# Experts' up rows in another order: two k of w1, then two of w3, before they alternate

## The chip, the core and the metric

The kernel runs on one core of a Trainium2 chip. The metric is the device time of one execution in microseconds (us); shorter is better. The time before is the median of three runs.

## The reference

One inference step of a small hybrid encoder, two layers, in float32. There are 512 prompt tokens and 8 x 16 sample tokens, 640 in all, of width 1024. Each layer mixes tokens (an mLSTM, a sparse attention with an indexer, a causal pooling) and then has a feed-forward part. In the first layer that is one dense SwiGLU. In the second it is a choice of two out of eight SwiGLU experts for each token, and this is where the change is:

```python
def _swiglu(x, wa, wb, wc):
    return (jax.nn.silu(x @ wa) * (x @ wb)) @ wc

logits = (x @ w_router).astype(f32) + b_router.astype(f32)
top_v, top_i = lax.top_k(logits, TOP_K)
gates = jax.nn.softmax(top_v, axis=-1)
comb = jnp.sum(jax.nn.one_hot(top_i, N_EXPERTS, dtype=f32) * gates[..., None], axis=1)
for e in range(N_EXPERTS):
    y = y + comb[:, e:e + 1] * _swiglu(x, we1[e], we3[e], we2[e]).astype(f32)
```

`we1` and `we3` are 1024 x 1408 for each expert, `we2` is 1408 x 1024.

## The kernel before

The engines run programs of their own, tied by semaphores; their order is written out by hand. The tokens are sorted by expert into passes of 128 slots. A pass is one expert's weights with up to 128 tokens. The number of passes is known only at run time. The first two `up()` and the last two `down()` stand outside of the loop; each trip of the loop (13 trips with these inputs, `trips`) does `down()` of one pass and then `up()` of the pass two further on.

Weights come as rows. An up row is 128 x 1408 floats (704 KB): one k of the 1024 inputs, in eights of 128, of w1 or of w3. There are `UP_ROWS` = 16 of them, and c counts them; before, c = 2k + which, with which = 0 for w1 and 1 for w3. A down row is 128 x 1024 (512 KB), `DOWN_ROWS` = 11. Each row passes through these stations, at a place of a ring of `NPLACE` = 9:

- SyncE fetches it (`expert_rows`, L636 to L648) into `expert_ring` once the place is free (`expert_used`).
- ScalarE rounds it to its upper part (`upper`, `copy` at L1708), into `region_split` for places 0 to 5 and into `z_weights_upper` for places 6 to 8.
- VectorE subtracts, which gives the lower part (`lower`, `tt` at L2295), in `expert_lower`, and counts `expert_split`.
- TensorE uses it. `weight_parts()` waits for `expert_split` once at the head of a row. `product` makes three matmuls: upper by upper, upper tokens by lower weights, lower tokens by upper weights.

ScalarE and VectorE work `AHEAD` = 4 rows before TensorE in the order of the program: at TensorE's row c their programs have row c + 4. Since 27 rows make a trip and 27 is three times 9, each row of the loop has the same place in each trip: up row c = 0 is in place 7, c = 1 in place 8, c = 2 in place 0.

In `up()` (TensorE, L1536) an up row is cut into three parts of 512, 512 and 384 columns (`PARTS`), and part p of the w1 rows adds into PSUM bank p, of the w3 rows into bank 3 + p. All k of a bank add up there. The first row that writes a bank calls `claim(b)`, which waits until the bank's last reader is done (`holder`).

In `down()` (L1557) the results go to banks 6 and 7, and in between TensorE transposes the next pass's products: `turn_product` for part 0 into bank 3 after f = 4, for part 1 into bank 4 after f = 8, for part 2 into bank 5 after the last row. ScalarE copies each out of its bank (`upper_of_product`), then VectorE subtracts (`lower_of_product`, L2946) into `region_split` and counts `product_split`; that frees the bank. VectorE's order at the end of a `down()` is: row split of up row 2, `lower_of_product` of bank 4, row split of up row 3, `lower_of_product` of bank 5; then `up()` goes on with up row 4. A place in the ring is freed by the first matmul of the row that follows (`free_place`).

Of the kernel before, what the change touches and what calls it, by code (L numbers as in the profile page):

```python
# [10 lines left out]
KD = D // P  # L11
# [16 lines left out]
NF = FE // P  # L28
# [46 lines left out]
UP_ROWS, DOWN_ROWS = 2 * KD, NF  # L75
PASS_ROWS = UP_ROWS + DOWN_ROWS
assert PASS_ROWS % NPLACE == 0
PARTS = [(0, 512), (512, 1024), (1024, FE)]
TRIPS_AT = 31
CHUNK_DMAS = [len(w) for _, w in UP_CHUNKS] + [1] * len(W2_CHUNKS)  # L80
# [105 lines left out]
def build(nc, a, c, o, d):  # L186
# [11 lines left out]
    with ctx:  # L198
# [354 lines left out]
        def _(sp):  # L553
# [13 lines left out]
            def rows(w):  # L567
                return w.rearrange("(k p) n -> p k n", p=P)
# [26 lines left out]
            for l in range(DEPTH):  # L595
                w = rows(a["w_in"][l, :, :])
# [8 lines left out]
                w = rows(a["w_out"][l, :, :])  # L605
# [5 lines left out]
                for _ in range(2):  # L611
                    with sp.Fori(0, 2) as i:
                        n.enter(i, {"weights_used": EXPERT_CHUNKS})
                        q0 = slots.count["q"]
                        w1, w3 = (a[x][l // 2, :, :].rearrange("(k p) (e n) -> e p k n", p=P, e=2) for x in ("w1", "w3"))
                        w2 = a["w2"][l // 2, :, :].rearrange("(e k p) n -> e p k n", p=P, e=2)
                        w1, w3, w2 = (x[bass.ds(i, 1), :, :, :].rearrange("e p k n -> p (e k) n") for x in (w1, w3, w2))
# [20 lines left out]
            def expert_rows(e, up):  # L638

                nonlocal q  # L640
                w1, w3, w2 = (x[bass.ds(e, 1), :, :, :].rearrange("e p k n -> p (e k) n") for x in by_row)
                for src in [w[:, k, :] for k in range(KD) for w in (w1, w3)] if up else [w2[:, f, :] for f in range(NF)]:
                    if q >= NPLACE:
                        sp.wait_ge(expert_used, n.value("expert_used"))
                    n.add("expert_used")
                    place = q % NPLACE
                    q += 1
                    sp.dma_start(ER[:, place, 0:src.shape[1]], src).then_inc(expert_in[place], 16)  # L648
# [194 lines left out]
        def _(pe):  # L843
# [5 lines left out]
            def wait(s, value):  # L849
                pe.wait_ge(s, value)  # L850
# [4 lines left out]
            def claim(*banks):  # L855
                for b in banks:
                    if holder[b]:
                        wait(*holder[b])
                        holder[b] = None
# [56 lines left out]
            k = KD + 2 * DEPTH  # L916
# [108 lines left out]
            for l in range(DEPTH):  # L1025
# [71 lines left out]
                for k in range(KD):  # L1097
                    take(z_hidden_split)
                    for name, rows, banks, Wf in lead:
                        if k == 0:  # L1100
                            take(weights_split)
                        w = [x[:, k, 0:rows] for x in Wf]
# [9 lines left out]
                for kind, chunk, name, part, banks, who in UNITS[2:]:  # L1112
# [8 lines left out]
                    if kind == "f":  # L1121

                        for k in range(KD):
                            w = [x[:, k, part * P:part * P + rows] for x in Wf]
# [130 lines left out]
                for u in range(PAIR_UNITS + 3):  # L1255
                    if u < PAIR_UNITS:
                        pair, t = divmod(u, NTP)
                        w = P * (t + 1)
# [235 lines left out]
                if l % 2:  # L1494
# [11 lines left out]
                    def weight_parts():  # L1506

                        nonlocal place
                        take(expert_split)
                        at = place % NPLACE  # L1510
                        place += 1
                        return expert_upper(at), ERL[:, at, :]
# [12 lines left out]
                    def turn_product(part, bank):  # L1525

                        first, end = PARTS[part]
                        wait(product_made, n.value("product_made") - 2 + part)
# [7 lines left out]
                    def up():  # L1536

                        wait(rows_split, n.value("rows_split"))
                        for c in range(UP_ROWS):
                            k, which = divmod(c, 2)  # L1540
                            w = weight_parts()
                            for part, (first, end) in enumerate(PARTS):
                                b = 3 * which + part
                                if k == 0:
                                    claim(b)
                                begin, ins = product(PS[:, b, 0:end - first], [x[:, k, :] for x in (XGH, XGL)],
                                                     [x[:, first:end] for x in w], k == 0, k == KD - 1)
                                free_place(begin)
                                if k == KD - 1:
                                    ins.then_inc((gates_summed, ups_summed)[which], 1)  # L1550
                                    made = (silu_made, product_made)[which]
                                    holder[b] = (made, n.add(made.name))
                            release[0] = True
                            if c == 9:
                                turn_rows(0, 6)
# [24 lines left out]
                    for u, unit in enumerate(LATE_ROWS):  # L1580
                        b = u % 6
                        claim(b)
                        for j in range(4):
                            if unit[0] == "gates":
                                if u == NT * 2 - len(EARLY_ROWS) + 2 and j == 0:
                                    wait(gates_spread, 1)
                                k = 4 * unit[2] + j
# [47 lines left out]
                for it in range(4):  # L1635
# [35 lines left out]
                    for j, blocks in enumerate(W2_CHUNKS):  # L1671
                        c = len(UP_CHUNKS) + j
# [28 lines left out]
        def _(act):  # L1701
            n = Tally()

            def take(s, inc=1):
                act.wait_ge(s, n.add(s.name, inc))
# [135 lines left out]
            for l in range(DEPTH):  # L1841
# [273 lines left out]
                if l % 2:  # L2115
# [16 lines left out]
                    def upper_of_product(part, bank):  # L2132

                        first, end = PARTS[part]
                        take(product_turned)
# [3 lines left out]
                    def up(following):  # L2139

                        for c in range(UP_ROWS):
# [4 lines left out]
                            if c == 10:  # L2146
                                upper_of_rows(0, 6)
                        for part, (first, end) in enumerate(PARTS):
                            take(gates_summed)
# [115 lines left out]
        def _(dve):  # L2265
# [114 lines left out]
            for l in range(DEPTH):  # L2380
# [545 lines left out]
                if l % 2:  # L2926
# [19 lines left out]
                    def lower_of_product(part, bank):  # L2946

                        first, end = PARTS[part]
                        fs = slice(first // P, end // P)
# [4 lines left out]
                    def up(following):  # L2954

                        for c in range(UP_ROWS):
# [4 lines left out]
                            if c == 10:  # L2961
                                lower_of_rows(0, 6)
                        for part, (first, end) in enumerate(PARTS):
                            take(silu_made)
# [186 lines left out]
```

## Time and profile before

| | |
|---|---|
| median of three runs | 2340.25 us (2330.97 to 2342.22) |
| the profiled execution | 2339.32 us |
| its span, first to last instruction | 2337.5 us |
| granted clock of TensorE, mean | 0.933 |
| TensorE busy | 2148.8 us, 92% |
| VectorE busy | 1470.3 us, 63% |
| ScalarE busy | 1146.3 us, 49% |
| moved by DMA | 485.87 MB, 208 GB/s over the span |
| experts' weight rows | 240 of 704 KB, 165 of 512 KB |

A profile is of one execution, and its times are microseconds from the first instruction. The granted clock is TensorE's share of full speed, 1.0 for 2.4 GHz and 0.5 for 1.2 GHz. The experts take the time from about 1520 to 2290 us. Matmuls overlap each other, so a matmul's duration is longer than the distance from its start to the start of the next one.

### The profile page before, as it was taken

What the parts mean: (1) busy time and instruction counts of PE and PEld (TensorE: products, weight loads), DVE (VectorE), ACT (ScalarE), POOL (GpSimd) and SP (SyncE); (2) the same over time, 40 slices, a digit from 0 to 9 for tenths busy, and PEclk for the clock granted to TensorE, in tenths of its full rate; (3) what the DMA queues carried; (4) which work ended last, traced back from release to release, by engine and by line L of the source; (5) the groups of instructions that cost most, each with busy time, mean ns of one, the idle gap of its engine ahead of it and who ended that gap; (6) DMA issues with size and microseconds to landing.
All of it is one profiled execution on the core that took longest, in us unless ns stands there. A gap on an engine that the chain in (4) does not pass through costs nothing.

```text
span 2337.5 us, 36949 instructions
## 1 busy us (share of the span) xinstructions
PE 2148.8 (92%) x14013; PEld 1849.1 (79%) x14013; DVE 1470.3 (63%) x2156; ACT 1146.3 (49%) x1589; POOL 173.1 (7%) x257
## 2 busy tenths in 40 slices
PE   6999878898999999989998879889999999999996
PEld 4999634598999999989985448778888878888883
DVE  3567544255545454566675425578888888888885
ACT  5421235444434333343212444367777777777773
POOL 3000120110000000000000211100001000000101
PEclk7999679898999999999996889899999999999998
DMA  9222465624545455522231743199999999999995
GB/s 318 60 73 71 135 223 187 226 82 110 163 135 163 135 162 137 160 80 69 73 100 26 239 150 123 58 338 348 367 359 354 356 374 358 380 363 352 347 364 198
DMA packets 285982, 485.87 MB, mean 208 GB/s; under 512 B 21791, under 2 KB 216873, under 8 KB 285857
## 3 DMA queue, kind: packets, MB, share of 16 engines
q1 hardware_dynamic: 265536, 418.72, 52.1%
q0 software_dynamic: 20320, 65.39, 8.0%
q8 instruction: 90, 1.47, 0.3%
q14 instruction: 36, 0.29, 0.0%
HBM read 456.23 MB, written 26.97 MB: 207 GB/s over the span
## 4 chain that ended last, share of the span: by engine, by line
PE 76%; DMA 10%; DVE 6%; ACT 4%; issue 3%; SPq 1%; POOL 1%; ACTq 0%; PEldq 0%; DVEq 0%; PEld 0%; POOLq 0%
PE banks L871 72%; DMA expert_ring<-in_we 5%; PE banks L875 3%; DMA weight_ring<-in_w_ada 2%; ACT region_split L1708 1%; DVE scratch L2295 1%; DVE region L2295 1%; ACT scratch L1708 1%; DVE expert_lower L2295 1%; DMA mix_t<-region 1%; DMA region<-region 1%; SPq L565 1%; DMA scratch<-bias_rows 0%; DVE region_split L2295 0%; ACT hidden_t L1708 0%
## 5 line engine op out<-in xcount | busy, mean ns | idle before, releaser
L2295 DVE TENSOR_TENSOR expert_lower<-expert_ring,region_split 128x1408 fp32r<-128x1408 f32 (+1 forms) x270 | 388.3, 1467 | 27.0 <-ACT region_split L1708 17.3
L871 PE MATMUL banks<-upper_parts,region_split 128*128 128x320 f32 x1664 | 390.7, 310 | 4.5 <-DVE upper_parts L2295 4.5
L871 PE MATMUL banks<-upper_parts,weights_lower 128*128 128x320 f32 (+1 forms) x1248 | 387.2, 310 | 0.0
L871 PE MATMUL banks<-region_split 128*128 128x320 f32 (+1 forms) x1376 | 375.7, 336 | 1.7 <-DVE upper_parts L2295 1.7
L1708 ACT ACTIVATE region_split<-expert_ring 128x1408 fp32r<-128x1408 f32 (+1 forms) x270 | 331.8, 1257 | 61.4 <-DMA expert_ring<-in_we 61.3
L871 PE MATMUL banks<-region_split,upper_parts 128*128 128x512 f32 (+1 forms) x996 | 302.9, 380 | 1.4 <-DVE upper_parts L2295 1.4
L871 PEld LDWEIGHTS banks<-upper_parts,region_split 128*128 128x128 f32 x1664 | 285.1, 189 | 4.8 <-issue 4.8
L871 PE MATMUL banks<-expert_lower,upper_parts 128*128 128x512 f32 x720 | 271.0, 376 | 0.0
L871 PE MATMUL banks<-z_weights_upper,upper_parts 128*128 128x384 f32 (+1 forms) x764 | 238.3, 344 | 24.0 <-DVE region_split L2295 23.9
L871 PEld LDWEIGHTS banks<-region_split 128*128 128x128 f32 x1376 | 244.0, 188 | 18.2 <-DVE upper_parts L2295 1.5
L2295 DVE TENSOR_TENSOR expert_lower<-expert_ring,z_weights_upper 128x1024 fp32r<-128x1024 f32 (+1 forms) x135 | 192.2, 1442 | 73.9 <-ACT z_weights_upper L1708 71.5
L871 PEld LDWEIGHTS banks<-upper_parts,weights_lower 128*128 128x128 f32 (+1 forms) x1248 | 235.3, 189 | 0.0
L2295 DVE TENSOR_TENSOR weights_lower<-weight_ring,region_split 128x2048 fp32r<-128x2048 f32 (+2 forms) x72 | 168.9, 2350 | 96.2 <-ACT region_split L1708 96.2
L1708 ACT ACTIVATE region_split<-weight_ring 128x2048 fp32r<-128x2048 f32 (+2 forms) x72 | 140.6, 1958 | 164.2 <-PE banks L871 162.5
L1708 ACT ACTIVATE region<-banks 128x320 f32<-128x320 f32 (+3 forms) x185 | 83.7, 468 | 271.5 <-PE banks L871 267.4
L1708 ACT ACTIVATE z_weights_upper<-expert_ring 128x1024 fp32r<-128x1024 f32 (+1 forms) x135 | 166.7, 1237 | 101.0 <-DMA expert_ring<-in_we 100.5
L871 PEld LDWEIGHTS banks<-region_split,upper_parts 128*128 128x128 f32 x996 | 188.3, 191 | 31.7 <-DVE upper_parts L2295 1.8
L871 PE MATMUL banks<-region_split,weights_lower 128*128 128x320 f32 x608 | 187.9, 309 | 0.0
L871 PE MATMUL banks<-upper_parts,z_weights_upper 128*128 128x320 f32 (+1 forms) x544 | 171.1, 314 | 11.2 <-DVE hidden_lower_parts L2295 10.1
L871 PEld LDWEIGHTS banks<-z_weights_upper,upper_parts 128*128 128x128 f32 x764 | 143.3, 188 | 48.2 <-DVE region_split L2295 35.0
L871 PE MATMUL banks<-hidden_lower_parts,z_weights_upper 128*128 128x320 f32 (+1 forms) x544 | 169.9, 312 | 0.0
L871 PEld LDWEIGHTS banks<-expert_lower,upper_parts 128*128 128x128 f32 x720 | 137.2, 191 | 20.2
(317 smaller groups left out, 3254.8 us busy)
## 6 DMA issues: line engine op xcount, KB each, us to landing
expert_ring<-in_we SPq DMA_DIRECT2D x240, 704.0 KB, 8.2
expert_ring<-in_we SPq DMA_DIRECT2D x165, 512.0 KB, 4.5
weight_ring<-in_w_ada SPq DMA_DIRECT2D x48, 1024.0 KB, 9.0
weight_ring<-in_w SPq DMA_DIRECT2D x88, 512.0 KB, 4.9
weight_ring<-in_w_in SPq DMA_DIRECT2D x24, 1024.0 KB, 5.3
weight_ring<-in_w SPq DMA_DIRECT2D x16, 1408.0 KB, 6.5
weight_ring<-in_w_out SPq DMA_DIRECT2D x8, 1024.0 KB, 6.5
y_rows<-hidden_t POOLq DMA_DIRECT2D x15, 512.0 KB, 7.5
```

Source lines behind the costliest of these rows:

```text
L565: sp.dma_start(dst, src).then_inc(weights_in[q % NSLOT], 16)
L871: return nc.tensor.matmul(out, lhsT, rhs, start=first, stop=last)
L875: return nc.tensor.transpose(out, in_, ident[0:k, 0:k])
L1708: return nc.scalar.activation(out, in_, f, **kw)
L2295: return v.tensor_tensor(out, x, y, op)
```

## The change

`UP_ORDER` lists (k, which) for each c. Rows c = 1 and c = 2 of each `up()` change places: before, the first four rows were (0, w1), (0, w3), (1, w1), (1, w3); after, they are (0, w1), (1, w1), (0, w3), (1, w3). From c = 4 on nothing differs. SyncE fetches in the new order, and TensorE computes in it. The order of k within each bank stays.

```diff
+UP_ORDER = [(0, 0), (1, 0), (0, 1), (1, 1)] + [(k, which) for k in range(2, KD) for which in range(2)]
...
-                for src in [w[:, k, :] for k in range(KD) for w in (w1, w3)] if up else [w2[:, f, :] for f in range(NF)]:
+                for src in [(w1, w3)[which][:, k, :] for k, which in UP_ORDER] if up else [w2[:, f, :] for f in range(NF)]:
                     if q >= NPLACE:
                         sp.wait_ge(expert_used, n.value("expert_used"))
...
                         for c in range(UP_ROWS):
-                            k, which = divmod(c, 2)
+                            k, which = UP_ORDER[c]
                             w = weight_parts()
                             for part, (first, end) in enumerate(PARTS):
                                 b = 3 * which + part
```

## Rows read from the trace of the kernel before

**Rows 1.** Page, part 1: engine busy us, share of span, instructions.

```profile
PE 2148.8 (92%) x14013; PEld 1849.1 (79%) x14013; DVE 1470.3 (63%) x2156; ACT 1146.3 (49%) x1589; POOL 173.1 (7%) x257
```

**Rows 2.** Page, part 4: chain that ended last, share of span by line.

```profile
PE banks L871 72%; DMA expert_ring<-in_we 5%; PE banks L875 3%; DMA weight_ring<-in_w_ada 2%; ACT region_split L1708 1%; DVE scratch L2295 1%; DVE region L2295 1%; ACT scratch L1708 1%; DVE expert_lower L2295 1%; DMA mix_t<-region 1%; DMA region<-region 1%; SPq L565 1%; DMA scratch<-bias_rows 0%; DVE region_split L2295 0%; ACT hidden_t L1708 0%
```

**Rows 3.** Page, part 5: group, count | busy, mean ns | idle before, releaser.

```profile
L871 PE MATMUL banks<-z_weights_upper,upper_parts 128*128 128x384 f32 (+1 forms) x764 | 238.3, 344 | 24.0 <-DVE region_split L2295 23.9
```

**Rows 4.** TensorE's waits, 1600 to 2260 us: total us, times, longest.

```profile
PE banks L871 <- DVE region_split L2295: 23.9, 24, 1.3
```

**Rows 5.** Stretches, one per pass: length, busy (count) by engine, clock, DMA share, GB/s.

```profile
1621.45:1671.82 50.37, 48.45 (x233) 40.55 (x231) 43.03 (x36) 38.01 (x37) 3.71 (x4) 1.00 0.96 366
1671.82:1723.74 51.92, 49.99 (x232) 41.76 (x231) 43.92 (x36) 38.58 (x38) 3.70 (x4) 0.97 0.96 356
1723.74:1773.27 49.53, 48.43 (x233) 40.55 (x231) 42.41 (x36) 37.27 (x38) 3.69 (x4) 1.00 0.97 369
...
1823.37:1874.12 50.75, 48.43 (x233) 40.57 (x230) 43.25 (x36) 37.85 (x38) 3.71 (x4) 1.00 0.96 364
...
1924.69:1976.79 52.10, 49.89 (x230) 41.74 (x230) 44.55 (x36) 38.74 (x38) 3.69 (x4) 0.97 0.95 355
...
2177.39:2229.10 51.71, 50.02 (x233) 41.80 (x231) 42.54 (x36) 37.53 (x37) 3.69 (x4) 0.97 0.94 351
sum 607.65, PE 585.82 PEld 490.19 DVE 516.13 ACT 453.57 POOL 44.33; mean PE 48.82 PEld 40.85 DVE 43.01 ACT 37.80 POOL 3.69
```

**Rows 6.** TensorE's timeline: start, us, instruction [idle before <-releaser].

```profile
1621.45 0.48 PE L871 MATMUL banks<-z_weights_upper,upper_parts 128*128 128x512 f32 x1
...
1625.19 0.51 PE L871 MATMUL banks<-z_weights_upper,upper_parts 128*128 128x512 f32 x1 [0.89 <-DVE region_split L2295]
...
1627.19 0.45 PE L871 MATMUL banks<-z_weights_upper,upper_parts 128*128 128x384 f32 x1 [1.03 <-DVE region_split L2295]
...
1627.84 0.39 PE L871 MATMUL banks<-region_split,upper_parts 128*128 128x512 f32 x1
1628.06 0.40 PE L871 MATMUL banks<-expert_lower,upper_parts 128*128 128x512 f32 x1
...
1629.98 0.39 PE L871 MATMUL banks<-expert_lower,upper_parts 128*128 128x512 f32 x1
...
1728.65 0.44 PE L871 MATMUL banks<-z_weights_upper,upper_parts 128*128 128x384 f32 x1 [1.04 <-DVE region_split L2295]
...
1778.77 0.45 PE L871 MATMUL banks<-z_weights_upper,upper_parts 128*128 128x384 f32 x1 [1.04 <-DVE region_split L2295]
...
1827.49 0.49 PE L871 MATMUL banks<-z_weights_upper,upper_parts 128*128 128x512 f32 x1 [1.27 <-DVE region_split L2295]
...
1829.49 0.45 PE L871 MATMUL banks<-z_weights_upper,upper_parts 128*128 128x384 f32 x1 [1.05 <-DVE region_split L2295]
```

**Rows 7.** ScalarE's and VectorE's timeline in the first pass, same columns.

```profile
1621.49 1.39 ACT L1708 ACTIVATE region_split<-expert_ring 128x1408 fp32r<-128x1408 f32 x1 [0.36 <-DMA expert_ring<-in_we]
...
1622.91 1.62 DVE L2295 TENSOR_TENSOR expert_lower<-expert_ring,region_split 128x1408 fp32r<-128x1408 f32 x1
...
1624.45 0.68 DVE L2295 TENSOR_TENSOR region_split<-banks,region_split 128x512 fp32r<-128x512 f32 x1
...
1625.05 1.61 DVE L2295 TENSOR_TENSOR expert_lower<-expert_ring,region_split 128x1408 fp32r<-128x1408 f32 x1
...
1626.58 0.55 DVE L2295 TENSOR_TENSOR region_split<-banks,region_split 128x384 fp32r<-128x384 f32 x1
...
1627.27 6.23 DVE L2295 TENSOR_TENSOR expert_lower<-expert_ring,region_split 128x1408 fp32r<-128x1408 f32 x4
```

**Rows 8.** Other stretches, columns as in rows 5.

```profile
1678.00:1681.50 3.50, 3.50 (x11) 2.92 (x11) 3.50 (x3) 3.15 (x3) 0.00 (x0) 0.53 1.00 410
...
1773.00:1797.00 24.00, 22.30 (x107) 18.71 (x106) 22.12 (x16) 19.95 (x19) 0.59 (x1) 1.00 1.02 416
1797.00:1816.00 19.00, 19.00 (x92) 16.04 (x91) 17.81 (x18) 14.82 (x17) 3.10 (x3) 1.00 0.85 285
```

## The prediction

> **What bounds the kernel now.** I read the page first. TensorE is busy 92% of the span, VectorE 63%, ScalarE 49% [rows 1], and the chain that ended last runs 72% through the one matmul line L871, with 5% on the experts' weight DMAs [rows 2]. So the time is TensorE's, wherever TensorE has something to do, and a change pays only where TensorE stands still. Among the costliest groups one names such a place: matmuls that read `z_weights_upper` with `upper_parts` (the tokens' upper parts, so an up row, held in a ring place from 6 to 8) had 24.0 us of idle time before them, released by VectorE writing `region_split` [rows 3]. The list of waits says that this is all there is: in the stretch of the expert loop TensorE waits for one thing alone, 24 times, 23.9 us in total [rows 4].
>
> The next view is the table by stretches, cut at the first matmul of each `up()` of the loop. It gives twelve whole passes of the expert loop (a thirteenth `up()` follows at 2229.10), 607.65 us together, 50.6 us on average, with TensorE busy for 48 to 50 us of each, VectorE for 42 to 45 and the DMA share at 0.94 to 0.97 [rows 5]. TensorE is the bound, but the DMA share is what can spoil a gain, and I come back to it.
>
> The timeline of one pass shows the wait itself. The pass starts at 1621.45. A row without a wait takes 1.92 us (1628.06 to 1629.98, the same matmul in two rows that follow each other), so the third row should start at 1621.45 + 0.09 (the first matmul after the transposes is that much longer) + 2 x 1.92 = 1625.38. It starts at 1627.84 [rows 6]. The lost time, about 2.5 us, has two stops, both *within* row c = 1: one before the matmuls of its second part, which go on at 1625.19, and one before its third, at 1627.19 [rows 6]. A stop between parts of a row can't be a wait for that row's weights, since `weight_parts()` waits once at the head of the row. It is `claim(b)` for banks 4 and 5. Row c = 1 is k = 0 of w3, and it opens banks 3, 4, 5. Their last holder is `turn_product`, whose banks come free when ScalarE has copied and VectorE has subtracted (`lower_of_product`, `product_split`).
>
> VectorE's own timeline shows why it is late. It splits row 2 at 1622.91 (ScalarE rounded it from 1621.49 on, and had waited for the DMA), then `lower_of_product` for bank 4 at 1624.45 with 0.68 us (ends 1625.13, TensorE goes on at 1625.19), then row 3 at 1625.05 with 1.61 us, then `lower_of_product` for bank 5 at 1626.58 with 0.55 us (ends 1627.13, TensorE goes on at 1627.19) [rows 7]. The releases sit in VectorE's queue behind row splits, and the splits behind the DMA. They come at a time that TensorE's work on row c = 1 does not set.
>
> **The change part by part.**
>
> *SyncE's queue.* The second and the third row of each `up()` are fetched in the other order: (k 1, w1) before (k 0, w3). Both are 704 KB rows. The number, size, ring place and order of places are the same, and so are the waits. Nothing is moved past another queue. Cost: nothing.
>
> *ScalarE and VectorE.* They work by place. Their instructions are the same ones in the same order. Cost: nothing. Their deadlines change: until now TensorE reached row c = 2 only after the stops; now it reaches it earlier.
>
> *TensorE.* Row c = 1 now adds k = 1 of w1 into banks 0 to 2, already open, and claims nothing. Banks 3, 4, 5 are claimed in row c = 2. From c = 4 on all is as before, and each bank's k order stays. The claim of bank 5 moves from 0.09 + 1.92 + 1.39 = 3.40 us after the pass starts to 5.32 us (1.39 is two parts of three matmuls, at 0.23 each, as between 1628.06 and the next row). Bank 4's goes to 4.62.
>
> What stands against it is when the banks come free, counted from the pass's start: in the first pass 3.7 us for bank 4 and 5.7 for bank 5; in the worst of the thirteen, the one from 1823.37, 4.1 and 6.1; in the mildest kind, the one from 1723.74, bank 5 at 4.9 [rows 5, 6]. So bank 4 never stops TensorE again (4.1 against 4.6). Bank 5 still does in most passes, by 5.7 - 5.3 = 0.4 us in the usual one, 0.8 in the worst, nothing in the mildest. Over the thirteen I count 6 us, 0.45 us each. The stall shrinks; it doesn't go.
>
> Next in line are the weights. Row 2's split ends 1624.53, 3.1 us after the start, and TensorE will want it at 3.9. Row 3's ends at 5.2, wanted at 5.8 or later. Row 4's ends at 1627.27 + 1.62, which is 7.4, wanted at 8.2 [rows 7]. From there VectorE makes a row in 1.56 us (6.23 for four) and TensorE uses one in 1.92, so the distance grows. In the worst pass all of these are 0.4 us later and still in time, because bank 5 holds TensorE back by as much. So nothing new is waited for, by 0.4 us or more.
>
> *The sum.* A pass without a stop is 50.37 - 2.55 = 47.82 us (first pass, third row at 1627.84 in place of 1625.29 with 3.84 for two rows; the small 0.09 is in both). With the 0.45 us that stay it is 48.3. Twelve passes: 607.65 - 12 x 48.3 = 28 us saved. The thirteenth `up()` saves 2. Together 30 us. That holds a gift: three of the passes are 51.7 to 52.1 us long, as the one from 1671.82, and in each the granted clock falls to the lower level directly behind the two stops (a mean of 0.53 from 1678.0 to 1681.5, that is 1.2 GHz for nearly all of this stretch; it is the first of three such) [rows 5, 8]. Each fall costs about 1.6 us (51.92 against 50.37). With one stop of 0.4 us in place of two of about 1 us I expect fewer of them, but not surely none. If all three stay, the sum is 30 - 5 = 25 us. I take 28. The profiled execution had 2339.3 us, the median of the three runs is 2340.25, so nothing is to be rescaled: 2340.25 - 28 = 2312.
>
> *The first two `up()`* before the loop have no such wait in row c = 1: banks 3 to 5 were drained long before by other work. Bounds for this part: 0 to 1 us either way; I take 0.
>
> **The transfers, which could take it back.** A pass moves 366 GB/s x 50.37 us = 18.4 MB [rows 5]. In 48.3 us that is 382 GB/s. Is that to be had? In the stretch 1773 to 1797 the queues were full (share 1.02) and moved 416 GB/s; from 1797 to 1816 they moved 285 GB/s at a share of 0.85 [rows 8]. In this second stretch TensorE frees a place every 1.92 us and gets a 512 KB row for it, so the queues are fed slowly. That leaves 19 x (416 - 285) = 2.5 MB, 6 us of transfer, unused in each pass. A pass that is 2.1 us shorter takes 2 of these 6, and the backlog is gone before the next pass's first up rows are asked for. By this, 18.4 MB need 44.2 us, and TensorE's 48.3 stay the bound. The share of 0.96 overstates how near the limit is.
>
> The Trainium skill, "SBUF — State Buffer" (its summary of rules for kernel authors), says to reckon with about 358 GB/s between HBM and SBUF, because the HBM side binds; by that alone a pass of 18.4 MB would take 51 us and this change would bring nothing. The passes here already run at 351 to 369 GB/s and the full stretch at 416 [rows 5, 8], so the trace speaks against that figure as a limit for this core. The Trainium skill, "HBM Reference" (its specifications), gives about 425 GB/s for a core that streams alone; with that the trace agrees.
>
> **The rivals.**
>
> *A. The rows land later, in part.* With less slack in the queues the first up rows arrive perhaps 1 us later against TensorE, and both VectorE's releases and its splits with them. Then 1.4 us a pass stay in place of 0.45. For it: ScalarE waits for the DMA before nearly each row, and the DMA is full from before the pass's start. Against it: the pass from 1723.74 lasted only 49.5 us, and the bank 5 release of the one behind it, which started at 1773.27, was at 5.5 us (1778.77), no later than usual [rows 5, 6]. Time: 13 x 1 us given back, 2325.
>
> *B. The transfers are the bound.* If the mean pass of 50.6 us is what the queues need, TensorE's stops only move to the heads of rows. Against it are the 6 us unused, and passes of 49.5 to 50.4 us beside that mean. Time: 2340, no change. (By the Trainium skill's figure of 358 GB/s, "SBUF — State Buffer", this would be the case.)
>
> *C. Slower.* As B, but the waiting now comes in the middle of the row sequence, just where TensorE had run undisturbed, and the clock falls behind it in each pass and not in three. Price: ten more falls at 1.6 us, 2340 + 16 = 2356. It decides from the point where row 2's split comes over 2 us later than now (after 5.5 us rather than 3.1).
>
> *D. More than forecast.* The bank 5 stop goes altogether, if splits run a little earlier, and no clock fall is left: 30 + 6 = 36 us, 2304.
>
> That the change doesn't do what it says I hold for excluded by the place of the stops (between parts of a row, ending 0.06 us behind the VectorE instruction that frees the bank).
>
> **How the numbers follow.** Forecast (2306 to 2320): 0.66. A: 0.17. B: 0.06. C: 0.03. D: 0.08. The predicted time is 2312. The range goes from D, with the scatter of the runs (2331 to 2342) in mind, at 2301, to A with half a us more per pass, at 2330. What a measurement of this kernel can tell from no change is about 0.5%, 12 us: faster takes the forecast, D and nearly all of A, 0.90; within takes B and the rest of A, 0.07; slower is C, 0.03.
>
> **What would show it.** In the profile after: the 24 waits of TensorE for `region_split` become about 11 to 13, each of 0.2 to 0.8 us, now before a matmul that reads `region_split` weights (row 2 sits in place 0) and none in the second part; passes of about 48.3 us; GB/s over 375 in the passes; clock falls behind the stops rarer than three. Wrong is the step on the transfers if TensorE then waits at heads of rows for `expert_lower`, or if passes stay at 50 us; wrong is the bank step if two stops a pass remain.

## The result and the profile after

The changed kernel takes 2301.86 us (median of four, 2295.37 to 2306.12); beside it the kernel before took 2337.51 us (median of four). The ratio is 0.9833, with an interval of 0.9800 to 0.9865. The medians are 35.6 us apart (the ratio makes it 39) where 28 were forecast, and 2301.9 stands against 2312: the direction and the place were right, the size was too small by a fifth or more. The profiled execution took 2302.05 us, with a span of 2300.2.

The page first, part 1, the matmul group of rows 3, and then the list of TensorE's waits in the expert loop, as in rows 4 (total us, times, longest; the view lists stops of over 0.15 us):

```profile
PE 2128.3 (93%) x14013; PEld 1843.0 (80%) x14013; DVE 1465.5 (64%) x2156; ACT 1142.4 (50%) x1589; POOL 222.9 (10%) x257
...
L872 PE MATMUL banks<-z_weights_upper,upper_parts 128*128 128x384 f32 (+1 forms) x764 | 230.4, 339 | 0.1
```

```profile
PE banks L872 <- DVE region_split L2296: 0.6, 1, 0.6
```

The 24.0 us of idle time ahead of that group are 0.1. Of 24 waits [rows 4] one is left. Part 1 holds a second thing that I had not looked for: GpSimd is busy for 222.9 us, where it was 173.1 [rows 1], with the same 257 instructions.

The stretches between the first matmuls of the loop's `up()` (length, busy and count of PE, PEld, DVE, ACT, POOL, clock, DMA share, GB/s), to be held against rows 5:

```profile
1618.99:1667.75 48.76, 48.20 (x229) 40.60 (x230) 44.19 (x36) 38.31 (x38) 6.77 (x4) 1.00 0.97 373
1667.75:1715.62 47.87, 47.87 (x233) 40.69 (x231) 42.56 (x35) 38.12 (x39) 7.92 (x4) 1.00 0.98 382
...
2146.49:2194.36 47.87, 47.87 (x233) 40.69 (x231) 42.72 (x35) 37.24 (x38) 7.75 (x4) 1.00 0.98 381
sum 575.37, PE 574.82 PEld 488.09 DVE 513.28 ACT 451.73 POOL 94.32; mean PE 47.90 PEld 40.67 DVE 42.77 ACT 37.64 POOL 7.86
```

Eleven of the twelve passes are TensorE's own work and nothing else: 47.87 us long (47.86 to 47.91), 47.87 us busy, at full clock. The twelve together went from 607.65 to 575.37 us, 32.3 less. After the first matmul of the last `up()` come 105.8 us in place of 108.4, and before the first one 1619.0 in place of 1621.5. Together that is the 37.3 us between the two spans.

### The profile page after: what moved, and what is told of

The parts are those of the page before. It is cut to its first block, busy times and chain, and to the rows that moved or that the text cites. A ratio compares the mean times of both kernels' runs of the same rounds, so it can differ in the third digit from the quotient of the medians.

```text
span 2300.2 us, 36949 instructions
## 1 busy us (share of the span) xinstructions
PE 2128.3 (93%) x14013; PEld 1843.0 (80%) x14013; DVE 1465.5 (64%) x2156; ACT 1142.4 (50%) x1589; POOL 222.9 (10%) x257
## 4 chain that ended last, share of the span: by engine, by line
PE 83%; DVE 5%; DMA 5%; ACT 3%; issue 2%; POOL 1%; ACTq 0%; PEldq 0%; DVEq 0%; PEld 0%; POOLq 0%
PE banks L872 78%; PE banks L876 4%; DMA weight_ring<-in_w_ada 1%; DVE scratch L2296 1%; DVE region L2296 1%; ACT scratch L1709 1%; DMA expert_ring<-in_we 1%; DMA mix_t<-region 1%; DMA region<-region 1%; ACT region_split L1709 1%; DMA scratch<-bias_rows 1%; ACT hidden_t L1709 1%; ACT region L1709 0%; DVE mix_t L2296 0%; DVE weights_lower L2296 0%
## 5 line engine op out<-in xcount | busy, mean ns | idle before, releaser
L872 PE MATMUL banks<-z_weights_upper,upper_parts 128*128 128x384 f32 (+1 forms) x764 | 230.4, 339 | 0.1
```

Source lines behind the costliest of these rows:

```text
L872: return nc.tensor.matmul(out, lhsT, rhs, start=first, stop=last)
```

## What had moved that the prediction held fixed

The one stop that is left is in the first pass. TensorE's timeline (start, us, instruction, idle before):

```profile
1622.91 0.39 PE L872 MATMUL banks<-region_split,upper_parts 128*128 128x512 f32 x1
...
1625.02 0.44 PE L872 MATMUL banks<-region_split,upper_parts 128*128 128x384 f32 x1 [0.56 <-DVE region_split L2296]
```

This is what was forecast for most passes: row c = 2 begins 3.9 us after the pass's start (1618.99), and its third part waits a little for bank 5, until 6.0 us. In the other passes bank 5 is free before it is claimed, and not because TensorE claims later than I said. To see why, take a pass from the middle of either kernel and look at GpSimd, VectorE and ScalarE. Before, the pass that starts at 1773.27:

```profile
1760.19 2.35 DVE L2295 TENSOR_TENSOR expert_lower<-expert_ring,region_split 128x1024 fp32r<-128x1024 f32 x2
1760.52 1.85 POOL L803 DMA_INDIRECT hidden_t<-h_rows,pass_tokens  x1 [0.52 <-issue]
...
1769.65 1.38 ACT L1708 ACTIVATE z_weights_upper<-expert_ring 128x1408 fp32r<-128x1408 f32 x1 [3.08 <-DMA expert_ring<-in_we]
...
1773.08 1.38 ACT L1708 ACTIVATE region_split<-expert_ring 128x1408 fp32r<-128x1408 f32 x1 [0.34 <-DMA expert_ring<-in_we]
```

After, the pass that starts at 1763.52:

```profile
1751.44 4.62 DVE L2296 TENSOR_TENSOR expert_lower<-expert_ring,region_split 128x1024 fp32r<-128x1024 f32 x4
1751.77 5.25 POOL L804 DMA_INDIRECT hidden_t<-h_rows,pass_tokens  x1 [0.53 <-issue]
...
1755.98 0.68 DVE L2296 TENSOR_TENSOR region_split<-banks,region_split 128x512 fp32r<-128x512 f32 x1
...
1757.79 1.38 ACT L1709 ACTIVATE z_weights_upper<-expert_ring 128x1408 fp32r<-128x1408 f32 x1 [1.49 <-DMA expert_ring<-in_we]
...
1762.13 1.38 ACT L1709 ACTIVATE region_split<-expert_ring 128x1408 fp32r<-128x1408 f32 x1 [0.82 <-DMA expert_ring<-in_we]
```

Both instructions on GpSimd are the token gather that each trip of the loop makes (`gather`, an indirect DMA of 512 KB; the reader finds it as `hidden_t<-h_rows,pass_tokens`). It starts about 12 us before the pass in both kernels. Before, it takes 1.85 us; after, 5.25, while VectorE splits four rows without a pause. The first up row is rounded 3.6 us before the pass's start in the kernel before (1769.65 against 1773.27) and 5.7 us before it in the changed one (1757.79 against 1763.52); row c = 2 at -0.2 and at -1.4.

The DMA view of the same stretches tells what stands between. Lines are queue, kind, packets, MB, share; q1 has SyncE's loads, q0 what GpSimd issues. Before, from 9.3 to 3.3 us ahead of the pass:

```profile
q1 hardware_dynamic: 317, 1.60, 72.0%
q0 software_dynamic: 144, 0.52, 24.1%
```

After, from 9.5 to 3.5 us ahead of the pass, where q0 has no line at all, and then from 3.5 us ahead to 0.5 us after its start:

```profile
q1 hardware_dynamic: 385, 1.92, 89.9%
```

```profile
q1 hardware_dynamic: 233, 1.17, 69.9%
q0 software_dynamic: 139, 0.52, 31.7%
```

The gather's 0.52 MB travelled ahead of the first up rows before. Now they travel behind the first two. These rows, and the bank releases that hang on them, come earlier. The first pass of the changed kernel, the one with the stop, fits in: there the gather took 1.83 us, its packets travelled from 9.5 to 3.5 us ahead of the pass, and ScalarE began on row c = 0 at -3.1. That made theory 1 for the experiments: *the place of the gather's traffic decides when the first up rows land and so when bank 5 is free*. Theory 2 is that the rows land earlier because the passes are shorter, and the gather only follows. Theory 3 is about the cause behind theory 1: *GpSimd's gather instruction stands behind VectorE's unbroken row splits* (a split is VectorE's subtraction for one row of weights).

## The experiments

In this table the loop's twelve passes go from the first matmul of its first `up()` to that of its last, in the profiled execution of each kernel. The last column is when ScalarE starts on row c = 0, against the pass's start, leaving out passes right behind a clock fall. Ratios are to the kernel before on the same chip in the same hours.

| kernel | median us | ratio to before (interval) | twelve passes us | row c = 0 |
|---|---|---|---|---|
| before | 2337.5 | 1 | 607.65 | -4.3 to -3.1 |
| changed | 2301.9 | 0.9833 (0.9800 to 0.9865) | 575.37 | -6.1 to -5.0, once -3.1 |
| e1 before, gather late | 2316.8 | 0.9911 (0.9879 to 0.9943) | 587.82 | -6.5 to -5.1 |
| e2 changed, plain load | 2299.8 | 0.9839 (0.9816 to 0.9861) | 574.89 | -5.2 to -3.7 |
| e3 before, plain load | 2329.7 | 0.9962 (0.9943 to 0.9981) | 599.57 | -4.6 to -3.5 |
| e4 before, products first | 2310.5 | 0.9889 (0.9859 to 0.9919) | 587.47 | -5.8 to -3.1 |
| e5 changed, gather late | 2304.5 | 0.9872 (0.9827 to 0.9917) | 574.47 | -6.3 to -5.1 |
| e6 three k of w1 first | 2303.0 | 0.9851 (0.9799 to 0.9903) | 574.78 | -6.4 to -3.9 |
| e7 changed, rows' part later | 2302.8 | 0.9864 (0.9811 to 0.9918) | 574.52 | -6.1 to -4.1 |
| e8 e6 and e7 together | 2303.7 | 0.9874 (0.9826 to 0.9921) | 574.54 | -5.9 to -3.1 |
| e9 changed, VectorE lets the gather through | 2303.8 | 0.9873 (0.9832 to 0.9915) | 578.67 | -4.5 to -3.1 |
| e10 e6 and e9 together | 2304.1 | 0.9869 (0.9816 to 0.9921) | 574.37 | -6.0 to -3.4 |

The whole times scatter by some 10 us within a kernel, so differences of a few microseconds are read in the twelve passes, not in the medians.

### Moving the gather alone, in the kernel before (e1)

```diff
                         pool.wait_ge(rows_turned, i * 2 + 6)
+                        pool.wait_ge(product_turned, i * 3 + 4)
                         gather(bass.ds(i + 3, 1), i + 4)
```

> The kernel before, with one more wait on GpSimd: in the loop it starts a pass's token gather only when TensorE has turned the first part of the products (after down row f = 4), about 5 us later than now. In the changed kernel the gather's packets travel from 4 us before the pass's start, behind the first two up rows; in the kernel before from 9 to 5 us before it, ahead of them. Theory 1 (the place of the gather's 0.5 MB in the queues decides when the first up rows land, and so when VectorE frees banks 4 and 5): here up rows c = 0 and 1 land 1.5 to 2 us earlier against TensorE, row 2 about 1 us earlier, the bank 5 release comes 0.5 to 1 us earlier, and with 13 passes the kernel is 7 to 13 us faster than before (2325 to 2331). Theory 2 (the rows land earlier in the changed kernel because its passes are shorter, the gather only follows): no change within 3 us.

2316.8 us against 2334.3 beside it, ratio 0.9911: 17 to 21 us faster without a change of TensorE's order. That is more than the 7 to 13 of theory 1 and outside anything that theory 2 allows. TensorE's waits in the loop:

```profile
PE banks L872 <- DVE region_split L2296: 10.3, 13, 1.6
```

10.3 us in 13 waits, against 23.9 in 24 [rows 4]: each pass still has its bank 5 stop and none has the bank 4 stop. I had undersized it. Row c = 2 came 1.5 to 2 us earlier and not 1, since most of the gather travelled behind this row as well; and none of the three clock falls of the kernel before (one is in rows 8) was left.

### The same load, early, by a plain DMA (e2 and e3)

```diff
+                        if plain:
+                            pool.dma_start(GR[:, :], d["h_rows"][0:P, :]).then_inc(gathered_in, 16)
+                            return
                         pool.indirect_dma_start(GR[:, :], None, d["h_rows"],
...
-                        gather(bass.ds(i + 3, 1), i + 4)
+                        gather(bass.ds(i + 3, 1), i + 4, True)
```

> The changed kernel; in the loop the indirect gather is replaced by a plain DMA of the same 512 KB (always the first 128 tokens' rows, so the experts' results are of other tokens; the amount of work is the same). Its GpSimd instruction took 0.6 us for the store of the same size, against 5.3 us for the gather, so its packets should travel early again, ahead of the first up rows. Theory 1: the up rows land as late as in the kernel before, the bank 5 stop comes back with 0.3 to 0.8 us a pass, passes of 48.2 to 48.5 us in place of 47.87, and the kernel takes 2306 to 2310. Theory 2: passes stay at 47.87, 2302.

> The kernel before with the same plain DMA in place of the gather in the loop (the experts' results are of other tokens). The control for the run on the changed kernel: here the gather's packets are early anyway. Theory 1: the two stops of a pass stay within 0.5 us in sum, 2331 to 2341. Theory 2: the same. If the kind of the gather mattered by itself (descriptors, 4 KB rows from scattered addresses), this would be faster by more than 8 us.

Neither came as written. In e2 I looked for the stop to come back; its twelve passes take 574.89 us, one of them 48.23 and the rest within 0.1 of 47.87, and no wait of TensorE is listed. In e3 the kernel before was to stay as it was; its twelve passes became 8 us shorter (5 us by the medians of the whole times, 9 by the ratio). GpSimd's instruction took 0.57 to 0.62 us in all passes of both, and so the packets travelled at about -11 to -6 us, 2 to 3 us ahead of where the gather's packets are in the kernel before. There the queues are not yet full (rows 8 show such a stretch: 285 GB/s). So this pair didn't test the old place of the gather. What it shows is that a load well ahead of the first up rows costs less than the gather at its old place (599.57 us against 607.65), and one behind them less still (e1, 587.82). Since e3 changes both the place and the kind of the load, it doesn't tell how much of its 8 us is the kind's, and its gain lies just where the expectation had put the border. That e2's rows land some tenths earlier than e3's, with the load at about the same place, is left without an explanation; it speaks for a part of theory 2.

### The queue on VectorE (e4)

```diff
                         for f in range(NF):
+                            if products and f in (5, 9):
+                                lower_of_product(f // 4 - 1, 2 + f // 4)
+                            if products and f == NF - 1:
+                                lower_of_product(2, 5)
                             if f + AHEAD < NF:
                                 lower(D)
...
-                            if products and f in (5, 9):
-                                lower_of_product(f // 4 - 1, 2 + f // 4)
-                        if products:
-                            lower_of_product(2, 5)
```

> The kernel before; VectorE's lower_of_product stands ahead of the row split of the same step in down(), not behind it. It tests the step on the place of the stops without touching TensorE's order. If the banks come free late because VectorE splits a row (1.6 us) ahead of each release, the bank 4 stop goes nearly altogether and bank 5 is released about 1 us earlier: 1.0 to 1.5 us less per pass, 13 to 20 us faster than before (2318 to 2325). Rival: ScalarE's copies are the late ones, and VectorE's order changes nothing: 2337.

2310.5 us against 2334.3 beside it, 24 to 26 us faster (medians, ratio). VectorE's order ahead of the releases was a cause of the stops, and ScalarE's copies alone were not. They come next: in e4 VectorE waits for the copy before it releases bank 4, and each release comes about 1.1 us earlier, though a split of 1.6 us is out of its way:

```profile
1761.81 0.69 DVE L2295 TENSOR_TENSOR region_split<-banks,region_split 128x512 fp32r<-128x512 f32 x1 [0.57 <-ACT region_split L1708]
```

The gain passes the forecast since in five of the thirteen passes the gather's instruction took 2.99 or 4.13 us in place of 1.85, went behind the first up row, and this row came at -5.8 to -5.1 and not at -4.0 to -3.1. So this run holds both states of the gather side by side: thirteen passes of one kernel, and the first up row is early in just those passes in which the instruction was slow.

### Holding the gather late in the changed kernel, and claiming later still (e5, e6)

e5 has the wait of e1. e6 changes one line:

```diff
-UP_ORDER = [(0, 0), (1, 0), (0, 1), (1, 1)] + [(k, which) for k in range(2, KD) for which in range(2)]
+UP_ORDER = [(k, which) for which in range(2) for k in range(3)] + [(k, which) for k in range(3, KD) for which in range(2)]
```

> The changed kernel with the wait of e1 (gather starts behind the first part's transpose). If the place of the gather's traffic is all that decides the remaining stop, this holds it behind the first two up rows by order and not by chance: 12 or 13 passes of 47.87 us without a stop, also the first, which had 0.56 us and 48.76; 2298 to 2304. Rival: the gather now lies in front of row c = 2 and delays it beyond 3.9 us after the pass's start, and stops at heads of rows appear: 2305 to 2315.

> The changed kernel, but three k of w1 first, then three of w3 (banks 3 to 5 claimed from c = 3 on, 1.9 us later still). Theory: in the changed kernel the loop's passes are TensorE's own 47.87 us, and only the first has a stop (0.56 us): at most 1 us to gain, 2297 to 2304. If anything else than the bank claims still held a pass up, it would show in passes other than 47.9 us.

Twelve passes: 574.47 and 574.78 us, within 1 us of the changed kernel's 575.37, which is the first pass's stop. Nothing is left to gain at this place: twelve times 47.87 is 574.4. The rival of e5 isn't borne out; the gather behind row c = 1 delays nobody. In e6 the first pass took 48.25 us: there a split was late, the one of row c = 8, which ended at 1644.10, and TensorE went on at 1644.16. This is a wait for a row, which the expectation had looked out for, in one pass of twelve. The medians of e5 and e6 differ from the changed kernel's by less than their scatter.

### Is the gather held by VectorE? (e7 and e8, then e9 and e10)

GpSimd's gather takes 1.06 us at its shortest (in e1, beside a VectorE that waits) and mostly 1.85, 2.99, 4.13 or 5.26 otherwise. The steps are 1.13 to 1.14, the distance from start to start of VectorE's splits of down rows (4.62 us for four of them). In the changed kernel it ends at 1757.02, which is 1.04 us after VectorE has turned, at 1755.98, from its four splits to an operation that reads PSUM. This fits an instruction that waits for a run of splits to end and then does its 1.06 us.

The kernel before shows that the end of the run isn't the whole rule. There the gather (1760.52, 1.85 us) ends at 1762.37, which is 1.05 us after the start of the second split of a pair that follows without a pause (1760.19, 2.35 us for both). It got in at the border between the two, in all thirteen passes. What differs is how long the second row had lain ready. ScalarE, before and after:

```profile
1759.03 2.00 ACT L1708 ACTIVATE region_split<-expert_ring 128x1024 fp32r<-128x1024 f32 x2
```

```profile
1749.28 2.00 ACT L1709 ACTIVATE region_split<-expert_ring 128x1024 fp32r<-128x1024 f32 x2
```

Before, it was rounded at 1761.03, 0.29 us ahead of its split; after, at 1751.28, 1.30 us ahead. In e4 the gather got in at this border in the eight passes with 0.29 to 0.32 us, and not in the five with 0.36 to 0.55. At later borders of a run as little as 0.11 us kept it out. So the gather is held while VectorE has a backlog of splits; what exactly lets it in stays open.

e7 puts VectorE's `lower_of_rows(1, 0)`, an operation on PSUM, at f == 2 and not at f == 1. e8 has e6's order besides.

> The changed kernel; VectorE's lower_of_rows(1, 0), which reads PSUM, stands one step later in down() (after three row splits, not two). In the changed kernel GpSimd's gather instruction takes 5.26 us in most passes against 1.85 before, in steps of 1.13 us, which is the pitch of VectorE's 1024-column splits, and it gets through when VectorE turns to an operation on PSUM. Theory 3 (the gather instruction stands behind VectorE's back-to-back row splits, and this is why its traffic goes behind the first up rows): here it gets through after 1 to 3 us, the traffic runs ahead of the up rows again, row c = 0 lands at -3 to -4 us and not -5.3 against the pass's start, and the bank 5 stop comes back with 0 to 0.6 us in most passes: 2300 to 2310, passes of 47.9 to 48.5. Rival (the instruction is slow for another reason, such as the DMA queues): 5.26 us and passes of 47.87 stay, 2302.

> e7 with three k of w1 first (as in e6). If what e7 loses is the claim of bank 5 alone, the claim at 7.2 us after the pass's start comes behind any release seen (4.0 to 6.1 us), and every pass is 47.87 us whatever the gather does: 2297 to 2304. Rival: with an early gather the rows themselves come late (stops at heads of rows), and passes stay over 48 us.

The gather did not go early: in e7 it took 4.11 to 4.13 us in eleven passes of thirteen. The run of splits behind the moved operation had three in it and no longer four, and the instruction became exactly one split's distance shorter (1.13 us); but GpSimd's copy of the token numbers ahead of it was now held for longer. One pass of e7, GpSimd and VectorE:

```profile
1748.37 2.97 POOL L800 COPY pass_tokens<-token_table 128x1 int32 x1 [28.09 <-PE banks L876]
...
1752.13 4.12 POOL L804 DMA_INDIRECT hidden_t<-h_rows,pass_tokens  x1 [0.53 <-issue]
```

```profile
1747.80 3.49 DVE L2296 TENSOR_TENSOR expert_lower<-expert_ring,region_split 128x1024 fp32r<-128x1024 f32 x3
1751.21 0.68 DVE L2296 TENSOR_TENSOR upper_parts<-banks,upper_parts 128x512 fp32r<-128x512 f32 x1
1751.81 3.48 DVE L2296 TENSOR_TENSOR expert_lower<-expert_ring,region_split 128x1024 fp32r<-128x1024 f32 x3
1755.21 0.68 DVE L2296 TENSOR_TENSOR region_split<-banks,region_split 128x512 fp32r<-128x512 f32 x1
```

The copy of 128 numbers takes 2.97 us and ends (1751.34) just behind the start of VectorE's PSUM operation (1751.21); the gather ends 1.04 us after the start of the next (1755.21). The lengths speak for theory 3, but the run didn't do what it was made for. In e8 the gather took 1.09 to 1.89 us in five passes of thirteen; in four of these row c = 0 came at -4.2 to -3.1, and still every pass took 47.87 us but one of 48.01, as expected of the later claim. e9 does in all passes what e7 was made for: VectorE itself waits until the gather is out (the setting up and counting of the semaphore `gather_issued` is left out here).

```diff
                         gather(bass.ds(i + 3, 1), i + 4)
+                        nc.gpsimd.tensor_tensor(NOTE[:, 1:2], ident[:, 0:1], ident[:, 0:1], ALU.add).then_inc(gather_issued, 1)
...
                             if rows and f == 1:
                                 lower_of_rows(1, 0)
+                                take(gather_issued)
```

> The changed kernel; VectorE, after two row splits and lower_of_rows(1, 0) in down(), waits until GpSimd has put out the pass's gather. Theory 3 (GpSimd's gather instruction stands behind VectorE's unbroken row splits): it now takes 1.0 to 1.9 us in all thirteen passes (5.26 in the changed kernel) and its packets travel at -9 to -4 us against the pass's start, ahead of the first up rows, as in the kernel before. Theory 1 (the place of this traffic decides when the first up rows land): row c = 0 is rounded from -3.0 to -4.3 us on and not from -5.3, and bank 5 stops TensorE again by 0.2 to 0.8 us in most passes, as the prediction had it: passes of 48.1 to 48.7 us, 2304 to 2311. Theory 2 (the shorter passes bring the rows in earlier by themselves): rows at -5 and passes of 47.87 stay, 2302.

> e9 with three k of w1 first. The rows land as late as in e9, but bank 5 is claimed 7.2 us after the pass's start, behind every release seen so far: passes of 47.87 us, at most one or two of 48.0, 2298 to 2304. If passes are longer than 48 us here, what the early gather costs is not the bank claim but the rows themselves.

In e9 the gather takes 1.06 to 1.08 us in all thirteen passes, nine tenths of its packets travel between -10 and -4.5 us (-8.6 to -4 in the kernel before), row c = 0 comes at -4.5 to -3.1, and the waits are back. That ScalarE waits 4.44 us for the transfer, in the lines below, shows that it is the row that lands late. GpSimd and ScalarE ahead of the pass that starts at 1904.91, then TensorE in it, then the stretch of this pass:

```profile
1892.59 1.07 POOL L805 DMA_INDIRECT hidden_t<-h_rows,pass_tokens  x1 [0.53 <-issue]
```

```profile
1901.79 1.38 ACT L1713 ACTIVATE z_weights_upper<-expert_ring 128x1408 fp32r<-128x1408 f32 x1 [4.44 <-DMA expert_ring<-in_we]
```

```profile
1911.04 0.44 PE L876 MATMUL banks<-region_split,upper_parts 128*128 128x384 f32 x1 [0.70 <-DVE region_split L2300]
```

```profile
1904.91:1953.77 48.86, 48.16 (x230) 40.61 (x230) 43.40 (x36) 37.84 (x39) 3.94 (x5) 1.00 0.97 377
```

Eleven of the twelve passes are longer than 47.87 (47.91 to 48.86), on average by 0.35 us: 578.67 - 12 x 47.87 = 4.2 us; only four of the stops are long enough to be listed. That is the 0.45 us a pass of the prediction, a little smaller. A small part of it is not the bank's: at the start of the pass from 1904.91 TensorE stood 0.08 us for the split of row c = 0. In e10 the rows come as late (-4.5 to -3.4 in twelve of thirteen passes), bank 5 is claimed one row later, and the twelve passes take 574.37 us without a wait. So an early gather costs nearly all that it costs through the bank claim, and theories 1 and 3 stand, 3 with what was said above of the borders. Of theory 2 some tenths are left, those named under e2 and as many here: row c = 0 comes at about -3.9 in e9 and at about -3.4 in the kernel before, with the gather at nearly the same place. In the medians this doesn't show: 4 us is less than their scatter.

The Trainium skill, "SBUF — State Buffer" (on who interferes with whom), states the cause in general: a VectorE instruction with two SBUF inputs contends with a GpSimd instruction that reads SBUF, and one with at most one SBUF input, outside its two-port modes, does not. The runs agree with it: the splits have two inputs in SBUF, the operations that let GpSimd through read PSUM, and the plain DMAs from GpSimd, which read no index from SBUF, took 0.53 to 0.62 us whatever VectorE did. That it is the reading of the index that is held up is likely by this, but no run tries it by itself. The page says that the one that issues first has the ports for its whole instruction; here GpSimd is also kept out at the border of two splits when the second has lain ready (5.26 us reaches over four of them), and gets in at such a border when it hasn't (1.85 us in the kernel before). The measurement decides.

## Why the prediction came out as it did

*What bounds the kernel, and where it stops*: right. With the claims of banks 3 to 5 out of row c = 1 both stops went in eleven passes of twelve, and nothing to speak of took their place at the heads of rows. That the second went altogether is not the order's doing alone, as e9 shows.

*A pass without a stop is 47.82 us*: measured 47.87.

*Next in line, the weights*: right for the changed kernel's rows 2 to 4. The tightest is row c = 0, which the prediction didn't look at: its split ended 0.06 us ahead of the first pass, and TensorE stood 0.15 us for it.

*Bank 4 never again, bank 5 by 0.45 us in most passes*: the first half right, the second wrong, and this is the step that failed. Its working is right for the releases as they stood: the changed kernel's first pass (0.56 us) and e9 (0.35 us a pass) show it. But it took the releases as fixed against the pass's start, and its walk through the queues has no entry for GpSimd, so the gather stood in it at nothing. It held one more of TensorE's stops for unavoidable because I followed VectorE's queue back to the DMA and stopped there. What stood in the DMA queues ahead of the rows was the gather, and when the gather enters depends on how densely VectorE works, which the change altered. That this fell out in the change's favour was luck: the prediction had no cause for it. In the kernel before VectorE still waited 0.91 us for TensorE before it multiplied the products, and came to the down rows with little piled up; after, it doesn't wait. VectorE's timeline, before and after:

```profile
1755.55 1.85 DVE L2295 TENSOR_TENSOR region<-region,banks 128x512 f32<-128x512 f32 x3 [0.91 <-PE banks L871]
```

```profile
1746.91 1.74 DVE L2296 TENSOR_TENSOR region<-region,banks 128x512 f32<-128x512 f32 x3
```

That the shorter pass is what closes those gaps is read from the timelines and wasn't tried by itself. In numbers, the 12 x 0.45 = 5.4 us that were to stay are 0.9 (first pass 48.76).

*The clock falls*: all three gone. I had taken off 2 us for falls that might stay.

*The transfers*: right, and more room than needed. The passes run at 373 to 387 GB/s, against the 382 worked out, and even so there is slack in the pass from 1763.5 (8 us at 282):

```profile
1763.50:1787.50 24.00, 24.00 (x118) 20.78 (x117) 21.50 (x15) 19.40 (x19) 0.59 (x1) 1.00 1.02 418
...
1795.00:1803.00 8.00, 8.00 (x41) 6.58 (x40) 8.00 (x10) 6.04 (x8) 5.61 (x3) 1.00 0.86 282
```

*Rival A* had the sign wrong: rows c = 0 and 1 came nearly 2 us earlier against the pass's start, and row c = 2 about 1 us, not later. *B* and *C* fell with it. *D* is what happened, in its mechanism (splits earlier, no stop, no fall) and nearly in its price, 36 us. It had 0.08, since I had no cause for it. The chance was too small for this reason: the timings around the place were tight to some tenths (5.7 against 5.3), and such a margin deserved as much weight on the side of a gain as rival A got on the other.

*The sum again, by the two profiles*: twelve passes 28.0 forecast, 32.3 measured; the last `up()` and what follows, 2 and 2.6; the falls, -2 and 0; the part ahead of the loop, 0 and 2.5. The last is not the change's doing as far as the runs tell: the loop's first pass starts anywhere from 1614.0 (e4) to 1628.5 us (e6) in profiles of kernels that are alike up to there, or nearly.

## What to carry to other kernels

A wait on a bank that is drained behind other queues' work can be shortened or removed, here at no cost that the runs show, by letting the accumulation that is already open go on for one step more. When a release time is used as a fixed number in a sum, follow it back through the DMA queue as well: what travels there ahead of the awaited transfer, who issues it, and whether the change moves that issuer. And a small load from GpSimd in the middle of a weight stream has good and bad places; moving it alone, by one wait, was worth some 20 us here.

## What the runs showed of the hardware that was not expected

The instruction of an indirect DMA on GpSimd took 1.06 us beside an idle VectorE and up to 5.26 us behind four row splits in succession, mostly in steps of one split (1.13 us). Two splits without a pause held it for only 0.8 us when the second's row had been ready for 0.3 us (1.85 us in all, the kernel before). A copy of 128 integers took 0.18 us at its shortest and up to 3.5 us (e8), and ended 0.12 to 0.13 us behind the start of VectorE's operation on PSUM. Plain DMAs from GpSimd stayed at 0.53 to 0.62 us.

The clock fell to its lower level three times in the loop of the kernel before, each time directly behind the two stops of a pass, of 0.65 to 1.17 us each ([rows 8] have the first of the three falls), and three times in e3, which keeps most of these stops (18.0 us in 22 waits). In the changed kernel and in all the others, with 0 to 10.3 us of listed waits in the loop, it never fell there. Two stops of 1.6 to 2.2 us together thus cost about 1.6 us more than their own length in these passes, though not in all: the longest pair, 2.3 us in the pass from 1823.37, had no fall behind it.
